# Two columns of a modulation as one-column products on TensorE in the opening of a transformer kernel

## The chip, the cores and the metric

The kernel runs on one core of a Trainium2 chip. The metric is the device time of one execution in microseconds. TensorE (PE) multiplies, VectorE (DVE), ScalarE (ACT) and GpSimd (POOL) do the rest, SyncE (SP) starts most transfers. Each engine works through its own queue in order and waits on semaphores for the others.

## What is computed

Two blocks over 256 tokens of 1024 channels. What matters here is the opening of the first, and the filter network of the second, which depends on no token and is computed at the very start:

```python
c_act = jax.nn.silu(c)
mod = c_act @ w_ada[l] + b_ada[l]                       # 1024 x 9216
(sh1, sc1, ga1, sh2, sc2, ga2, sh3, sc3, ga3) = jnp.split(mod, N_MOD, axis=-1)
h = modulate(rms_norm(x, g_pre_ff1[l]), sh1, sc1)       # h * (1 + scale) + shift
f = swiglu(h, w1_gate[l], w1_up[l], w1_down[l])
...
h = jnp.sin(sin_freq[0] * (z @ w1 + b1))                # filter network, 256 positions
h = jnp.sin(sin_freq[1] * (h @ w2 + b2))
h = jnp.sin(sin_freq[2] * (h @ w3 + b3))
h = (h @ w_out).reshape(L, HYENA_ORDER, 2, HYENA_WIDTH)
h = h * jnp.exp(-t[:, None, None, None] * jnp.abs(decay))
```

The filters' spectra follow, and their scale from the sums of squares. sh1 and sc1 are the "first two columns" of the modulation: without them the first feed-forward stage can't start. All weights are 32-bit numbers; each large product is made of three (high times high, high times low, low times high), for which ACT makes the high part of every weight panel (L184), and DVE the low part (L190).

## The kernel before

The order of all work is written out by hand, engine by engine; there is no planner. The opening has two tasks side by side.

The first is the modulation. `w_ada` comes as 72 panels of 128x1024 (512 KB), eight for each of its nine columns of 1024. SP loads the first 16 panels (columns sh1 and sc1) into a ring of five slots (L2345, in `load_ada`). DVE multiplies each by one value of `c_act` per partition and adds it to one of two accumulators, `acc0` (L739 for the first of a column, L731 for the others); the helper `spare()` puts one such addition wherever the order of the filter work leaves a place. At the end PE sums `acc0` over partitions: `sum_columns` (L769) takes each 128x128 piece as weights, and a column of ones as the moving operand. DVE adds the bias (L781, L783), makes two diagonal matrices with the tokens' norms (`diag_dve`, L375), and PE turns X with them (`norm_pe`, L431) into banks 4 to 7. ACT scales the result (`norm_act_rest`, L329), and DVE makes its low part (`low_dve`, L393 and L395), channel by channel. With those the first feed-forward stage starts (`first_up`, its products all at L206).

The second is the filter network, `spectrum_pe`, `spectrum_dve`, `spectrum_act` and `spectrum_pool`: three small layers (L1132, L1129) with their argument on DVE (L1162 to L1165, `round_off` at L881 to L884) and the sine on ACT (L1211); eight products for the taps (L1141, two times four, the network's 64 channels as rows); the taps times their decay (L1184), their sums and differences on POOL and DVE (L1252, L1199), squares on ACT (L1234) and their sums (L1258 to L1260, then `filter_sums_pe`, L1117); then two transforms, o = 0 and o = 1, of four quarters each (L1153), copied by ACT (L1243) and stored. Between the first and the second network layer stand the parameters of a state-space part (`params_dve`, 24 small DVE instructions), and behind the third `params_rest_dve` (L907 to L934, 21 of them).

In the first feed-forward stage (`ffn_pe`, `ffn_act`, `ffn_dve` with n = 0) DVE also adds up five further columns of the modulation (`ada_add_middle`, L731 again), for which POOL first clears accumulators and loads a row (`ada_middle_pool`, L837 and L827), and POOL makes tables from the parameters (`tables_pool`). One column sum in `ada_middle_pe`, at the end of the stage, is the same L769.

A product of 32-bit numbers that isn't made of three is two instructions in the trace (an LDWEIGHTS and a MATMUL each).

Of the kernel before, what the change touches and what calls it, by code (L numbers as in the profile page):

```python
# [81 lines left out]
def build_program(nc, panels, ada, cols, rows, sinks, ssm_mats, skip, tables, pool_mats, rope, near,  # L82
                  pool_w, decay, mlp_w, feats, x_in, out, spectrum, last_stage):
    ctx = ExitStack()
    with ctx:
# [40 lines left out]
        acc0 = region(4096, 2, D)  # L126
# [180 lines left out]
        def norm_act_squares(act, n, lo=0, hi=4):  # L307
            if n == 0:
                act.wait_ge(x_loaded, 16)
# [97 lines left out]

        def norm_pe(pe, n, first):
# [19 lines left out]
            for m in range(MT):  # L428
                pe.wait_ge(diag_done, 2 * n + m + 1)
                for k in range(KT):  # L430
                    mm = pe.matmul(turned_out(n, k)[:, m * P:(m + 1) * P], X[:, m, k * P:(k + 1) * P],  # L431
                                   diag[:, m, :], start=True, stop=True)
                    if m == MT - 1:
                        mm.then_inc(turned, 1)
# [30 lines left out]
        def ffn_pe(pe, n):  # L465
# [36 lines left out]

            norm_pe(pe, at, first_up)
            up(1)
            down(0, start=True)
# [73 lines left out]
        def ffn_dve(dve, n, order):  # L579
# [38 lines left out]
            dve_panels(dve, base + 3, 2)  # L618
            hidden(0)
# [114 lines left out]
        def ada_add(dve, a, dst):  # L734

            slot, k = a % ADA_RING, a % KT
            dve.wait_ge(ada_loaded[slot], 16 * (a // ADA_RING + 1))
            if k == 0:
                dve.tensor_scalar(dst, ada_ring[:, slot, :], c_act[:, 0:1], None,  # L739
                                  ALU.mult).then_inc(ada_used, 1)  # L740
            else:
                ada_multiply_add(dve, a, dst, ada_ring[:, slot, :], c_act[:, k:k + 1])

# [29 lines left out]
        def ada_first_pe(pe):  # L773
            for c in range(2):
                pe.wait_ge(ada_used, 8 * c + 8)
                sum_columns(pe, acc0[:, c, :], 7, 8 * c).then_inc(column_sums, 1)

        def ada_first_dve(dve, order):
            dve.wait_ge(column_sums, 2)
            for j in range(2):  # L780
                order(dve.tensor_tensor(mods[:, j, :], bank[7][:, 8 * j:8 * j + 8],  # L781
                                        col("b_ada", 8 * j, 8), ALU.add))
# [30 lines left out]
        def ada_middle_dve(dve, order):  # L813
            dve.wait_ge(column_sums, 6)
# [71 lines left out]
        def params_dve(dve, order):  # L886
# [3 lines left out]
            order(dve.tensor_scalar(pr(T2), pr(T0), 1.0 / 40320, None, ALU.mult))  # L890
            for n in (7, 6, 5, 4, 3, 2, 1):
                order(dve.scalar_tensor_tensor(out=pr(T2), in0=pr(T2), scalar=1.0 / math.factorial(n),
                                               in1=pr(T0), op0=ALU.add, op1=ALU.mult))
            order(dve.tensor_scalar(pr(T1), pr(T1), -126.0, 127.0, ALU.max, ALU.min))
            order(dve.tensor_scalar(pr(DT).bitcast(I32), pr(T1), 127.0, 8388608.0, ALU.add, ALU.mult))
# [211 lines left out]
        tap_sq = [region(at, 512) for at in (24576, 25088, 25600, 1024)]  # L1107
        decay_rows = region(0, 1024)
# [4 lines left out]
        def filter_sums_pe(pe, o):  # L1113

            pe.wait_ge(squares_added, o + 1)
            for c in range(4):
                mm = pe.matmul(bank[6][:, 4 * o + c:4 * o + c + 1], tap_sq[0][:, c * P:(c + 1) * P],  # L1117
                               ones[:, 0:1], start=True, stop=True)
# [3 lines left out]
        SPEC_BANKS = (1, 2, 3, 0)  # L1122

        def spectrum_pe(pe):
            pe.wait_ge(spec_loaded, 16 * 2)
            for layer in range(3):
                if layer:
                    pe.wait_ge(mlp_sin, layer)
                    pe.matmul(bank[7][0:64, 0:SEQ], mlp[0:64, 256 + 64 * layer:320 + 64 * layer],  # L1129
                              mlp_h, start=True, stop=True).then_inc(mlp_product, 1)  # L1130
                else:
                    pe.matmul(bank[7][0:64, 0:SEQ], mlp[0:33, 256:320], feat_t,  # L1132
                              start=True, stop=True).then_inc(mlp_product, 1)
            pe.wait_ge(mlp_sin, 3)
            pe.wait_ge(spec_loaded, 16 * 5)
            for o in range(2):
                for q in range(4):
                    m, d = q // 2, q % 2
                    if (o, q) == (1, 3):
                        pe.wait_ge(taps_done, 1)  # L1140
                    pe.matmul(bank[TAP_BANKS[o][q]][:, :], mlp_h[:, m * P:(m + 1) * P],  # L1141
                              filter_out[0:64, o * 1024 + d * 512:o * 1024 + d * 512 + 512],
                              start=True, stop=True).then_inc(taps_product, 1)
            for o in range(2):
                if o:
                    filter_sums_pe(pe, 0)
                pe.wait_ge(even_odd, 4 * o + 4)
                for q in range(4):

                    pe.wait_ge(*((spec_done, q + 1) if o else (taps_done, (2, 3, 4, 8)[q])))  # L1150
                    f, s = q // 2, q % 2
                    for m in range(MT):
                        mm = pe.matmul(bank[SPEC_BANKS[q]][:, :], dft[:, s, m, f * P:(f + 1) * P],  # L1153
                                       eo[:, 2 * m + s, :], start=m == 0, stop=m == MT - 1)
                    mm.then_inc(spec_product, 1)
            filter_sums_pe(pe, 1)

        def spectrum_dve(dve, order, spare):

            for layer in range(3):  # L1160
# [6 lines left out]
                if layer == 0:  # L1167
                    params_dve(dve, order)
                    dve.wait_ge(c_ready, 1)
                else:  # L1170
                    spare()
            params_rest_dve(dve, order)
            for _ in range(3):
                spare()
            for o in range(2):
                for q in range(4):
# [3 lines left out]
                    if o:  # L1180
# [4 lines left out]
                                            decays[:, m, d * 512:d * 512 + 512], ALU.mult)  # L1185
# [5 lines left out]
                    if q == 1:  # L1191
                        spare()
                for _ in range(3 * o):
                    spare()
                dve.wait_ge(taps_done, 4 * o + 4)
                if o:
                    dve.wait_ge(spec_product, 4)
# [3 lines left out]
                for _ in range(3):  # L1201
                    spare()
# [1449 lines left out]
```

## Time and profile before

| | |
|---|---|
| median of 3 runs | 1668.34 us (1663.57 to 1670.28) |
| profiled execution, its own time | 1668.2 us |
| its span in the profile | 1666.5 us |
| TensorE busy in the span | 1562.0 us (94%) |
| first product of the first feed-forward stage | at 79.50 us |

The profile is one execution. Its page gives busy times and the chain of work that ended last; the trace behind it can be asked for stretches, groups of instructions and single ones. Times are from the start of the span.

### The profile page before, as it was taken

What the parts mean: (1) busy time and instruction counts of PE and PEld (TensorE: products, weight loads), DVE (VectorE), ACT (ScalarE), POOL (GpSimd) and SP (SyncE); (2) the same over time, 40 slices, a digit from 0 to 9 for tenths busy, and PEclk for the clock granted to TensorE, in tenths of its full rate; (3) what the DMA queues carried; (4) which work ended last, traced back from release to release, by engine and by line L of the source; (5) the groups of instructions that cost most, each with busy time, mean ns of one, the idle gap of its engine ahead of it and who ended that gap; (6) DMA issues with size and microseconds to landing.
All of it is one profiled execution on the core that took longest, in us unless ns stands there. A gap on an engine that the chain in (4) does not pass through costs nothing.

```text
span 1666.5 us, 28244 instructions
## 1 busy us (share of the span) xinstructions
PE 1562.0 (94%) x10274; PEld 1423.6 (85%) x10274; DVE 1035.7 (62%) x1378; ACT 755.0 (45%) x1193; POOL 229.7 (14%) x278
## 2 busy tenths in 40 slices
PE   4899999887899999999999999999999989999997
PEld 1598999777689998999988689999999978889996
DVE  6789775783465565655556865555655557665554
ACT  3344553434454444544454354444444445454443
POOL 1479137370010000100000000000000000000000
PEclk9799999885899999999999999999999998999999
DMA  6688785421246654755543345554655533255551
GB/s 221 227 337 287 277 291 194 151 79 38 89 164 219 209 208 146 284 189 189 186 140 120 123 150 185 184 184 149 215 181 185 180 110 100 68 175 189 188 180 48
DMA packets 80279, 293.11 MB, mean 176 GB/s; under 512 B 9035, under 2 KB 9388, under 8 KB 79644
## 3 DMA queue, kind: packets, MB, share of 16 engines
q1 hardware_dynamic: 74432, 270.71, 48.4%
q0 software_dynamic: 4864, 19.35, 3.2%
q10 hardware_dynamic: 924, 2.25, 0.5%
q8 instruction: 39, 0.64, 0.2%
q14 instruction: 20, 0.16, 0.0%
HBM read 289.13 MB, written 3.15 MB: 175 GB/s over the span
## 4 chain that ended last, share of the span: by engine, by line
PE 85%; DVE 6%; ACT 4%; POOL 2%; issue 2%; DMA 1%; ACTq 0%; DVEq 0%; POOLq 0%
PE bank L206 75%; DVE w_lo L190 1%; PE bank L769 1%; PE bank L1793 1%; PE bank L431 1%; DVE arena L731 1%; POOL arena L1590 1%; ACT arena L301 1%; PE bank L2122 1%; PE bank L1806 1%; PE bank L1421 1%; PE bank L1153 1%; PE bank L404 1%; PE bank L2144 1%; DVE arena L671 0%
## 5 line engine op out<-in xcount | busy, mean ns | idle before, releaser
L206 PE MATMUL bank<-h_hi,w_hi 128*128 128x256 f32 x2376 | 685.3, 288 | 9.5 <-DVE h_lo L2252 3.0
L206 PE MATMUL bank<-h_lo,w_hi 128*128 128x256 f32 x2376 | 677.3, 285 | 0.0
L206 PE MATMUL bank<-h_hi,w_lo 128*128 128x256 f32 x2376 | 676.9, 285 | 0.0
L190 DVE TENSOR_TENSOR w_lo<-raw,w_hi 128x1024 fp32r<-128x1024 f32 x458 | 548.8, 1247 | 104.2 <-ACT w_hi L184 101.4
L206 PEld LDWEIGHTS bank<-h_hi,w_hi 128*128 128x128 f32 x2376 | 460.9, 194 | 22.6 <-DVE h_lo L395 5.0
L184 ACT ACTIVATE w_hi<-raw 128x1024 fp32r<-128x1024 f32 x458 | 456.8, 1049 | 36.6 <-PE bank L206 32.3
L206 PEld LDWEIGHTS bank<-h_lo,w_hi 128*128 128x128 f32 x2376 | 461.0, 194 | 5.5 <-issue 1.0
L206 PEld LDWEIGHTS bank<-h_hi,w_lo 128*128 128x128 f32 x2376 | 460.6, 194 | 0.0
L596 DVE TENSOR_TENSOR arena<-arena,bank 128x256 f32<-128x256 f32 x132 | 55.4, 420 | 265.1 <-PE bank L206 180.7
L206 PE MATMUL bank<-w_hi,f_hi 128*128 128x512 f32 x528 | 207.3, 393 | 0.0
L206 PE MATMUL bank<-w_hi,f_lo 128*128 128x512 f32 x528 | 207.0, 392 | 0.0
L206 PE MATMUL bank<-w_lo,f_hi 128*128 128x512 f32 x528 | 205.5, 389 | 0.0
L544 ACT ACTIVATE f_hi<-arena 128x256 fp32r<-128x256 f32 x132 | 55.2, 418 | 238.7 <-DVE arena L596 238.7
L336 POOL TENSOR_SCALAR stat<-stat 128x1 f32<-128x1 f32 x26 | 9.7, 374 | 1049.5 <-ACT arena L301 1048.7
L538 ACT ACTIVATE arena<-arena 128x256 f32<-128x256 f32 x88 | 36.8, 418 | 196.2 <-DVE arena L590 196.2
L206 PEld LDWEIGHTS bank<-w_lo,f_hi 128*128 128x128 f32 x528 | 99.2, 188 | 21.6
L206 PEld LDWEIGHTS bank<-w_hi,f_hi 128*128 128x128 f32 x528 | 99.7, 189 | 17.2
L206 PEld LDWEIGHTS bank<-w_hi,f_lo 128*128 128x128 f32 x528 | 99.7, 189 | 15.8
L731 DVE SCALAR_TENSOR_TENSOR arena<-arena,stat 128x1024 f32<-128x1024 f32 x70 | 100.2, 1431 | 1.2
L601 DVE TENSOR_TENSOR f_lo<-arena,f_hi 128x256 fp32r<-128x256 f32 x132 | 59.2, 448 | 52.2 <-ACT f_hi L544 52.2
L542 ACT ACTIVATE arena<-bank 128x256 f32<-128x256 f32 x44 | 16.9, 384 | 156.0 <-PE bank L206 156.0
L206 PE MATMUL bank<-w_hi,h_hi 128*128 128x512 f32 x116 | 48.6, 419 | 7.0 <-DVE h_lo L1714 2.8
(316 smaller groups left out, 1370.2 us busy)
## 6 DMA issues: line engine op xcount, KB each, us to landing
raw<-panels SPq DMA_DIRECT2D x458, 512.0 KB, 4.5
arena<-ada SPq DMA_DIRECT2D x56, 512.0 KB, 4.8
arena<-ada POOLq DMA_DIRECT2D x16, 512.0 KB, 3.9
spectrum<-arena POOLq DMA_DIRECT2D x2, 1024.0 KB, 7.7
arena<-rows POOLq DMA_DIRECT2D x4, 512.0 KB, 4.2
arena<-spectrum POOLq DMA_DIRECT2D x1, 2048.0 KB, 18.7
X<-x_in SPq DMA_DIRECT2D x1, 1024.0 KB, 5.1
arena<-decay ACTq DMA_DIRECT2D x2, 512.0 KB, 6.5
```

Source lines behind the costliest of these rows:

```text
L184: act.activation(w_hi[:, slot, :], raw[:, slot, :], ACT.Copy).then_inc(hi_ready, 1)
L190: dve.tensor_tensor(w_lo[:, slot, :], raw[:, slot, :], w_hi[:, slot, :].bitcast(F32), ALU.subtract).then_inc(lo_ready, 1)
L206: last = pe.matmul(out_ap, a, b, start=start and n == 0, stop=stop and n == 2)
L301: return act.activation(squares[:, q, :], source, ACT.Square, scale=D ** -0.5, accum_out=stat[:, at + q:at + q + 1])
L404: tr = pe.transpose(turned_out(n, k)[:, m * P:(m + 1) * P], X[:, m, k * P:(k + 1) * P], ident[:, :])
L431: mm = pe.matmul(turned_out(n, k)[:, m * P:(m + 1) * P], X[:, m, k * P:(k + 1) * P], diag[:, m, :], start=True, stop=True)
L538: act.activation(ffn_buf[:, f % 2, :], gate_buf[:, f % 2, :], ACT.Silu).then_inc(silu_done, 1)
L542: act.activation(ffn_buf[:, f % 2, :], gate_out(at, f), ACT.Silu).then_inc(silu_done, 1)
L544: act.activation(f_hi[:, f % 2, :], ffn_buf[:, 2 + f % 2, :], ACT.Copy).then_inc(f_hi_done, 1)
L596: dve.tensor_tensor(ffn_buf[:, 2 + f % 2, :], ffn_buf[:, f % 2, :], up_out(at, f), ALU.mult).then_inc(hidden_done, 1)
L601: dve.tensor_tensor(f_lo[:, f % 2, :], ffn_buf[:, 2 + f % 2, :], f_hi[:, f % 2, :].bitcast(F32), ALU.subtract).then_inc(f_lo_done, 1)
L731: dve.scalar_tensor_tensor(out=dst, in0=src, scalar=c, in1=dst, op0=ALU.mult, op1=ALU.add).then_inc(ada_used, 1)
```

## The change

The first two columns no longer go through DVE. For each of the 16 panels, as soon as it is loaded, PE takes its eight 128x128 pieces as weights and the column of `c_act` as the moving operand, and writes 128 single columns into bank 6; at the end one DVE reduction adds them up by eights. These products are spread over `spectrum_pe`: panels 0 and 1 behind the first layer, 2 to 4 behind the second, 5 to 7 behind the third, 8 and 9 behind the taps of o = 0, 10 to 12 ahead of the last tap product of o = 1, 13 to 15 behind the second to fourth quarter of the first transform.

The parameters on DVE are cut in three (`params_dve_0` ahead of the first layer, `_1` and `_2` behind the first and second), and their rest moves into the first feed-forward stage, behind its second group of splits. X is turned between the two transforms (`norm_turn_pe`), and ACT scales it and splits three panels ahead of the second squares and copies. The second transform uses banks 0, 1 and 2. The network's inputs, and the identity, go from ACT's queue to SP's, ahead of X; both rows of the decay are loaded early and have their own place. The sums of squares of the second filter come behind `first_up`.

```diff
-        def ada_first_pe(pe):
-            for c in range(2):
-                pe.wait_ge(ada_used, 8 * c + 8)
-                sum_columns(pe, acc0[:, c, :], 7, 8 * c).then_inc(column_sums, 1)
+        def ada_first_pe(pe, lo, hi):
+            for a in range(lo, hi):
+                slot, c, k = a % ADA_RING, a // KT, a % KT
+                pe.wait_ge(ada_loaded[slot], 16 * (a // ADA_RING + 1))
+                if a == 0:
+                    pe.wait_ge(c_ready, 1)
+                for j in range(KT):
+                    at = KT * (KT * c + j) + k
+                    mm = pe.matmul(bank[6][:, at:at + 1], ada_ring[:, slot, j * P:(j + 1) * P],
+                                   c_act[:, k:k + 1], start=True, stop=True)
+                mm.then_inc(ada_used, 1)
...
         def spectrum_pe(pe):
             pe.wait_ge(spec_loaded, 16 * 2)
@@
                     pe.matmul(bank[7][0:64, 0:SEQ], mlp[0:64, 256 + 64 * layer:320 + 64 * layer],
                               mlp_h, start=True, stop=True).then_inc(mlp_product, 1)
+                    ada_first_pe(pe, 3 * layer - 1, 3 * layer + 2)
                 else:
                     pe.matmul(bank[7][0:64, 0:SEQ], mlp[0:33, 256:320], feat_t,
                               start=True, stop=True).then_inc(mlp_product, 1)
+                    ada_first_pe(pe, 0, 2)
@@
                     if (o, q) == (1, 3):
+                        ada_first_pe(pe, 10, 13)
                         pe.wait_ge(taps_done, 1)
                     pe.matmul(bank[TAP_BANKS[o][q]][:, :], mlp_h[:, m * P:(m + 1) * P],
                               filter_out[0:64, o * 1024 + d * 512:o * 1024 + d * 512 + 512],
                               start=True, stop=True).then_inc(taps_product, 1)
+                if o == 0:
+                    ada_first_pe(pe, 8, 10)
             for o in range(2):
-                if o:
-                    filter_sums_pe(pe, 0)
                 pe.wait_ge(even_odd, 4 * o + 4)
                 for q in range(4):
 
-                    pe.wait_ge(*((spec_done, q + 1) if o else (taps_done, (2, 3, 4, 8)[q])))
+                    pe.wait_ge(*((spec_done, (4, 4, 4, 5)[q]) if o else (taps_done, (2, 3, 4, 8)[q])))
@@
                     mm.then_inc(spec_product, 1)
-            filter_sums_pe(pe, 1)
+                    if o == 0 and q:
+                        ada_first_pe(pe, 12 + q, 13 + q)
+                if o == 0:
+                    pe.wait_ge(taps_done, 8)
+                    pe.wait_ge(mods_done, 1)
+                    norm_turn_pe(pe, 0)
+                    filter_sums_pe(pe, 0)
...
+            if n == 0:
+                pe.wait_ge(spec_done, 8)
             norm_pe(pe, at, first_up)
+            if n == 0:
+                filter_sums_pe(pe, 1)
             up(1)
+            if n == 0:
+                pe.wait_ge(filter_sums, 1)
             down(0, start=True)
...
             dve_panels(dve, base + 3, 2)
+            if n == 0:
+                params_rest_dve(dve, order)
+                filter_sums_dve(dve)
             hidden(0)
...
+            act.wait_ge(decay_done, 4)
+            squares_of(0)
+            params_act(act)
+            params_rest_act(act)
+            copies(0)
+            act_panels(act, 0, 3)
+            norm_act_rest(act, 0)
+            act.wait_ge(tap_sums, 1)
+            squares_of(1)
+            act.wait_ge(spectrum_stored, 16)
+            copies(1)
...
             sp.dma_start(C[:, :], cols).then_inc(small_loaded, 16)
+            sp.dma_start(feat_t, feats).then_inc(spec_loaded, 16)
+            sp.dma_start(mlp_ws, mlp_w[:, 0:192]).then_inc(spec_loaded, 16)
+            sp.dma_start(ident[:, :], tables[0]).then_inc(x_loaded, 16)
             sp.dma_start(X[:, :, :], x_in.rearrange("(m p) d -> p m d", p=P)).then_inc(x_loaded, 16)
```

## Rows read from the trace of the kernel before

**Rows 1.** The page: busy time, share of the span and instructions of each engine.
```profile
PE 1562.0 (94%) x10274; PEld 1423.6 (85%) x10274; DVE 1035.7 (62%) x1378; ACT 755.0 (45%) x1193; POOL 229.7 (14%) x278
```

**Rows 2.** Stretches: busy us (instructions) of PE, PEld, DVE, ACT, POOL; granted clock; DMA.
```profile
0.00:79.50 79.50, 49.45 (x135) 27.27 (x135) 55.00 (x104) 27.25 (x47) 24.30 (x24) 0.89 0.69 235
79.50:100.00 20.50, 20.50 (x148) 19.00 (x149) 16.50 (x26) 12.11 (x17) 8.92 (x9) 1.00 0.57 199
100.00:160.00 60.00, 57.03 (x400) 53.24 (x399) 56.69 (x46) 28.01 (x39) 56.72 (x42) 1.00 0.93 334
```

**Rows 3.** The chain of waits to 150 us: start, us, what.
```profile
2.00 5.83 DMA arena<-mlp_w
...
66.33 5.53 PE bank L769 x32
...
79.50 61.27 PE bank L206 x432
```

**Rows 4.** Groups by line and form, 0 to 79.5 us: busy us, mean ns.
```profile
L731 DVE SCALAR_TENSOR_TENSOR arena<-arena,stat 128x1024 f32<-128x1024 f32 x14 | 22.0, 1569 | 0.7
...
L739 DVE TENSOR_SCALAR arena<-arena,stat 128x1024 f32<-128x1024 f32 x2 | 2.5, 1243 | 0.0
```

**Rows 5.** Timeline of PE, instructions merged: start, us, count.
```profile
23.18 14.02 PE L1141 MATMUL bank<-arena 64*128 64x512 f32 x16 [3.00 <-ACT arena L1211]
39.93 7.30 PE L1153 MATMUL bank<-arena 128*128 128x512 f32 x12 [2.74 <-POOL arena L1252]
...
66.20 5.65 PE L769 MATMUL bank<-ones,arena 128*128 128x1 f32 x32
...
267.07 8.74 PE L769 MATMUL bank<-ones,arena 128*128 128x1 f32 x64
```

**Rows 6.** Narrow stretches of PE's changes of pace, columns as in rows 2.
```profile
39.90:43.90 4.00, 3.97 (x5) 1.83 (x6) 3.90 (x3) 0.28 (x1) 3.92 (x2) 1.00 0.38 131
43.90:47.20 3.30, 3.30 (x8) 1.14 (x6) 3.14 (x5) 0.00 (x0) 2.00 (x2) 1.00 0.80 210
...
66.20:67.60 1.40, 1.40 (x15) 1.40 (x14) 0.17 (x1) 1.40 (x4) 0.00 (x0) 1.00 0.83 278
67.60:71.90 4.30, 4.25 (x21) 4.16 (x20) 0.02 (x1) 0.20 (x1) 2.61 (x3) 0.51 1.02 379
72.70:77.90 5.20, 5.20 (x24) 5.20 (x25) 0.15 (x1) 0.52 (x2) 0.00 (x0) 0.50 0.04 16
...
272.00:273.00 1.00, 1.00 (x9) 1.00 (x8) 0.00 (x0) 0.00 (x0) 1.00 (x2) 0.72 0.00 0
```

**Rows 7.** Transfers of the first 12 us: GB/s in 40 slices; X, us to landing.
```profile
GB/s 0 0 0 0 0 0 92 106 344 337 188 273 423 410 410 410 382 423 410 396 399 394 436 409 382 410 396 410 423 423 423 396 410 396 396 410 423 423 423 410
...
X<-x_in SPq DMA_DIRECT2D x1, 1024.0 KB, 5.1
```

**Rows 8.** Timeline of all engines, 0 to 66 us: one layer, table, parameters, copies.
```profile
2.59 1.28 ACT L2407 ACT_TABLE_LOAD   x1 [2.59 <-issue]
...
16.17 0.53 DVE L1162 TENSOR_SCALAR arena<-bank,C 64x256 f32<-64x256 f32 x1
...
18.60 0.42 ACT L1211 ACTIVATE arena<-arena 64x256 f32<-64x256 f32 x1 [1.92 <-DVE arena L1165]
...
28.07 0.17 DVE L934 TENSOR_TENSOR par<-par 128x16 f32<-128x16 f32 x1
...
53.91 2.04 ACT L1243 ACTIVATE arena<-bank 128x512 f32<-128x512 f32 x4
```

**Rows 9.** Timelines around the start of the first stage.
```profile
86.71 0.28 PE L206 MATMUL bank<-h_hi,w_hi 128*128 128x256 f32 x1
86.83 0.28 PE L206 MATMUL bank<-h_lo,w_hi 128*128 128x256 f32 x1
...
86.91 0.39 ACT L542 ACTIVATE arena<-bank 128x256 f32<-128x256 f32 x1 [2.57 <-PE bank L206]
...
96.89 3.50 DVE L190 TENSOR_TENSOR w_lo<-raw,w_hi 128x1024 fp32r<-128x1024 f32 x3 [2.27 <-DMA arena<-rows]
```

More of the change, by code:

```diff
@@ L406, in turn_pe, with norm_turn_pe @@
                 tr.then_inc(turned, 1)
+        def norm_turn_pe(pe, n):
+            for m in range(MT):
+                pe.wait_ge(diag_done, 2 * n + m + 1)
+                for k in range(KT):
+                    mm = pe.matmul(turned_out(n, k)[:, m * P:(m + 1) * P], X[:, m, k * P:(k + 1) * P],
+                                   diag[:, m, :], start=True, stop=True)
+                    if m == MT - 1:
+                        mm.then_inc(turned, 1)
         def norm_pe(pe, n, first):
@@ L427, in norm_pe @@
                 return
[L428 to L434, printed above, removed]
+            if n:
+                norm_turn_pe(pe, n)
             for k in range(KT):
@@ L771, in sum_columns @@
             return mm
[L773 to L782 removed]
+        def ada_first_pe(pe, lo, hi):
[9 more added lines that the diff above has]
+                mm.then_inc(ada_used, 1)
+        def ada_first_dve(dve, order):
+            dve.wait_ge(ada_used, ADA_FIRST)
+            order(dve.tensor_reduce(mods[:, 0:2, :].rearrange("p c j -> p (c j)"),
+                                    bank[6][:, 0:ADA_FIRST * KT].rearrange("p (n k) -> p n k", k=KT),
+                                    AX.X, ALU.add))
+            first = mods[:, 0:2, :].rearrange("p c j -> p (c j)")
+            order(dve.tensor_tensor(first, first, col("b_ada", 0, 16), ALU.add))
             dve.scalar_tensor_tensor(out=pre_scale[:, 0, :], in0=mods[:, 1, :], scalar=1.0,
@@ L1166, in spectrum_dve @@
                                   ALU.max).then_inc(mlp_arg, 1)
[L1167 to L1174, printed above, removed]
+                if layer < 2:
+                    params[layer + 1](dve, order)
+            diag_dve(dve, 0)
             for o in range(2):
@@ L1190, in spectrum_dve @@
                     ins.then_inc(taps_done, 1)
[L1191 to L1194, printed above, removed]
                 dve.wait_ge(taps_done, 4 * o + 4)
                 if o:
+                    ada_first_dve(dve, order)
                     dve.wait_ge(spec_product, 4)
@@ L1200, in spectrum_dve, with load_decay, magnitudes @@
                                       ALU.subtract).then_inc(even_odd, 1)
-                for _ in range(3):
-                    spare()
         def filter_sums_dve(dve):
             dve.wait_ge(tap_sums, 2)
-            dve.tensor_copy(filter_scale, bank[6][:, 0:8]).then_inc(filter_sums, 1)
+            dve.tensor_copy(filter_scale, bank[3][:, 0:8]).then_inc(filter_sums, 1)
+        def load_decay(act, o):
+            act.dma_start(decay_rows[:, o, :], decay[o:o + 1, :].partition_broadcast(P)).then_inc(
+                decay_loaded, 16)
         def spectrum_act(act, order):
+            def magnitudes(o):
+                act.wait_ge(decay_loaded, 16 * (o + 1))
+                if o == 0:
+                    load_decay(act, 1)
+                return act.activation(decay_rows[:, o, :], decay_rows[:, o, :], ACT.Abs)
             for layer in range(3):
@@ L1271, in spectrum_pool @@
             store(1)
+            ada_middle_pool(pool, order)
             pool.wait_ge(filter_sums, 1)
@@ L2402, in _ @@
             order = Order(act, act_order)
[L2403 to L2407 removed]
+            load_decay(act, 0)
             act.wait_ge(spec_loaded, 32)
@@ L2412, in _ @@
             act.dma_start(dft[:, 1, :, :], pool_mats[5]).then_inc(spec_loaded, 16)
-            act.dma_start(decay_rows, decay[0:1, :].partition_broadcast(P)).then_inc(decay_loaded, 16)
+            act.wait_ge(small_loaded, 16)
+            act.activation(c_act, col("c", 0, 8), ACT.Silu).then_inc(c_ready, 1)
             norm_act_squares(act, 0)
             spectrum_act(act, order)
-            norm_act_rest(act, 0)
             for at, (kind, n) in enumerate(stages):
@@ L2432, in _ @@
             order = Order(dve, dve_order)
-            ada_next = iter(range(ADA_FIRST))
-            def spare():
-                a = next(ada_next, None)
-                if a is not None:
-                    ada_add(dve, a, acc0[:, a // KT, :])
-            dve.wait_ge(small_loaded, 32)
-            spectrum_dve(dve, order, spare)
-            for _ in range(ADA_FIRST):
-                spare()
+            dve.wait_ge(small_loaded, 16)
+            spectrum_dve(dve, order)
             dve_panels(dve, 0, 3)
-            filter_sums_dve(dve)
-            ada_first_dve(dve, order)
-            diag_dve(dve, 0)
             low_dve(dve, 0, order)
```

76 lines of the change are left out of this document (27 added, 49 removed).

## The prediction

> **What bounds the kernel now.** I began with the page, which says that TensorE is busy for 94% of the span [rows 1], so time outside it can only be won where it waits. The table by stretches shows where that is: from 79.5 us to 160 us PE is all but always busy, and ahead of 79.5 us for 49.5 of 79.5 us [rows 2]. The chain of waits then names what sets the length of this opening: first the small weights of the filter network, whose transfer takes 5.8 us, then much of DVE's work, and at the end 5.5 us of column sums on PE (L769), after which the first 432 products of the first feed-forward stage follow in one piece [rows 3]. So the question is when the first product L206 can start (79.50 us now) and what is then still late. DVE spends 22.0 + 2.5 us on the sixteen additions [rows 4]. The reader should also see, in the timeline of PE, that a piece of work there has two prices: twelve 128x512 instructions took 7.3 us in one stretch, the first ones 0.85 us each, and sixteen 64-row ones took 14.0 us, 0.85 us each [rows 5]. The stretches show five instructions in 4.0 us before 43.9 us and, after it, eight in 3.3 us, overlaps counted [rows 6]. That is 1.2 and 2.4 GHz. The granted-clock column says 1.00 on both sides of 43.9 us, so for the first 44 us I go by the pace of the instructions and not by that column; from 66 us on the two agree.
>
> **The small products.** Each of the 16 panels of the first two columns now costs PE eight products of 128x128 weights and one moving column, two instructions each: 16 instructions. The kernel has the same shape in L769 and L1117. At 2.4 GHz they went 13 in the 1.40 us from 66.20, that is 0.108 us each; at 1.2 GHz 20 in the 4.3 us to 71.90, that is 0.213 us each [rows 6]. A panel is 1.73 us or 3.41 us, all sixteen 27.6 or 54.6 us. What goes is 24.5 us of DVE and 5.65 us of PE [rows 4, 5]. So the sign of the change hangs on the clock. What the engine did: it had the full clock after a dense stretch (L1153), and then it fell to 0.50 at about 67.6 us, some 2 us into the one-column products; in the run of 64 at 267.07 it fell after 5.4 us (a mean of 0.72 from 272 to 273 us), and these 64 took 8.74 us, not 6.9 [rows 5, 6]. In the opening it has not risen by 37.2 us, although the 64-row products filled 14 us of PE; it rises 4.0 us into the 128x512 products [rows 5, 6]. In the changed kernel nothing but one-column products, the small network layers and the 64-row products runs ahead of the first spectrum product. I therefore take 1.2 GHz up to there, and 2.4 GHz as the other bound.
>
> The Trainium skill ("TensorE: Matmul & The Clock Gate", the section on why this matters for your kernels) asks to keep TensorE continuously busy to get the full clock. Taken by busy time alone it would give the full clock early on, and so the other sum, the first rival below; the two falls in [rows 6] speak against reading it so.
>
> **The new order, step by step.** *Start.* The network's two inputs now go ahead of X. Their transfer takes 5.8 us with X's 1 MB ahead of it [rows 3], which is 2.5 us at the 0.4 MB a us of [rows 7]; with half of that (decay) beside it instead, the network should start near 6 us, not at 7.96 us. That gain is not kept: PE next wants the first panel. X lands at 6.4 us now; 0.5 MB of decay rows ahead of it and a panel behind it, at about 0.4 MB a us [rows 7], give 9.0 us (bounds 8 and 11). Silu, which the first panel's product waits for, stands behind ACT's wait for the two inputs, three issues of DMAs and its table (1.28 us [rows 8]); I estimate it done near 8 us, and it matters only past 9 us. The sines of the parameters move behind the exponentials on ACT, which then may load a table again (1.28 us); ACT waits for PE there, so nothing.
>
> *Up to the spectrum (1.2 GHz).* From 9.0 us PE has 13 panels (44.3 us), two layers at 1.1 us (2.2), and eight tap products at 2 x 0.85 us (13.7): it ends at 69.2 us, the 60.2 us behind the 9.0. Does it wait for another? A layer on DVE and ACT takes from 16.17 to 19.02 us, 2.9 us [rows 8], and PE has two or three panels (6.8 or 10.2 us) beside it: no. A panel's transfer of 1.3 us hides behind 3.41 us of product. The three parts of the parameters cost DVE what they cost before, but DVE is now idle there: nothing.
>
> *First spectrum.* It starts at 39.93 us in the kernel before [rows 5] and at 69.2 us in the changed one. Two quarters are 6.8 us at 1.2 GHz; with the clock rising after 4.0 us as now, 5.4 us. Two more at 1.7 us and panels 13 to 15 at 1.73 us: 8.6 us. PE is at 83.2 us. If the clock rises only after these it is 93.1 us, which I keep for the range.
>
> *Modulation and turning.* DVE's reduction, addition and product (about 0.2 us each, and 0.85 us lie between the last column sum and the first turning product now: 71.85 and 72.70 us) with the hand-over take 0.9 us: 84.1 us. The 32 turning instructions ran 5.2 us at 1.2 GHz before the clock rose [rows 6], at 0.21 us each, after a run of one-column products; the nearest row is this one, so 5.2 us for 24 and 0.8 us for the rest: 6.0 us (3.4 us if the clock holds). The sums of the first filter are eight more one-column instructions, 0.9 us: 91.0 us. The second spectrum, 16 instructions at 0.427 us, takes 6.8 us: 97.8 us, and its last copy on ACT (2.04 us for four [rows 8]) lets PE go at 98.4 us.
>
> *Who else could be late.* From their like in [rows 8]: ACT has three splits (3.3 us) from 82, the scaling (behind the turning, to 92), the squares (2.2 us) and then the copies: the first is done near 95, a bit ahead of where bank 0 is wanted. DVE subtracts 2.4 us, splits three panels (3.7 us with POOL quiet) and makes the low parts at 0.92 us each from about 90 us: done at 97.5 us. Both are just hidden; each late microsecond would show. It helps that the scaling (norm_act_rest) now comes ahead of the second squares and copies on ACT.
>
> *Start of the first stage.* The low parts are there, so the 48 first instructions go at 0.12 us instead of DVE's 0.92 us for six [rows 9]: 5.8 us, from 98.4 to 104.2 us; then the second filter sums, 0.9 us: 105.1 us. They end now at 86.8 us, just ahead of their first use on ACT at 86.91 [rows 9]. The end moves by +18.3 us.
>
> *Behind it.* The 21 instructions of the parameters' rest (4.5 us from 23.73 to 28.24 us) [rows 8] move to DVE between the splits and the first hidden tile; queued behind them are that tile and the splits of three panels, and PE waits for the tile in the down product. DVE reaches them some 4 us earlier against PE than before, and loses the 2.27 us that it now waits for the accumulators' rows [rows 9]. So nothing; at worst 4.5 us, since DVE is busy for 56.7 of the 60 us from 100 us on [rows 2]. POOL's tables wait for these parameters, the pow and the memsets, and start at about the same distance from the stage's start. Zero, between -2 and +4.5 us.
>
> **Sum.** The profiled execution took 1668.2 us (span 1666.5 us), as the median of 1668.34 us. 1668.2 + 18.3 = 1686.5; I predict 1686 us.
>
> **The rivals.** *Full clock early* (0.09): being busy without a gap suffices and the panels cost 1.73 us each from about 9 us. It saves 13 x 1.68 us, 1.1 us of layers, 6.8 us of taps, 2.0 us in the first spectrum and 2.6 us in turning, less about 1 us for landings: 33.4 us, 1653 us, faster. For it: PE has no gap. Against: both falls during such products [rows 6]. It decides if the clock rises before panel 5: from there on 18 us are saved.
> *Clock up with the first taps* (0.10): these run behind a full PE now, not behind a gap. Saved from 42.4 us on: taps 4.8, panels 8 to 12 8.4, first spectrum 2.0, together 15.3 us: 1671 us, no change to be told. Against: 14 us of these very products didn't raise it [rows 5].
> *Never up in the first spectrum, or DVE the bound behind it* (0.05 beyond my range): 83.2 becomes 93.1 us, and with 4.5 us of parameters and 2 us of a later start it is 1703 us.
> *PE at 1.2 GHz* as summed has 0.76: from 1681 us (turning at full clock, -2.6 us, first panel at 8 us, -1, and the -2 us behind the start) to 1702 us.
>
> **How the numbers follow.** Likeliest 1686 us. The range from 1670 to 1702 us reaches down to the case of the taps (half of its 0.10 lies in it) and leaves out the early full clock and the slow end, 0.19 in all. About 0.5% (8 us) can be told from no change by this measurement. Faster 0.10 (the early full clock, and 0.01 of the taps' case if it falls well), same 0.11 (the rest of the taps' case and 0.02 of mine, if two of its small gains meet others that I don't see), slower 0.79 (0.74 of mine and the 0.05 of the slow end).
>
> **What would show it.** Right: PE instructions of panels 0 to 12 some 0.21 us apart, the layers two and three at about 16 and 27 us, first spectrum product near 69 us, first L206-like product near 98 us, DVE idle through much of the first 65 us. Wrong: a pace of 0.11 us in the panels, which takes the whole sum down; a first stage that starts well before 90 us; or a new gap of PE behind the second spectrum or between 105 and 160 us.

## The result and the profile after

The changed kernel takes 1694.7 us (median of four runs, 1690.15 to 1698.42) against 1668.28 us (four runs, 1663.57 to 1670.28): a ratio of 1.0166, 95% interval 1.0138 to 1.0194. It is slower, by 26 us in the medians and by 22.0 us in the two profiled executions (1690.15 against 1668.2 us). Two single runs of other kernels below, one of 5251.48 us (experiment 6) and one of 4826.04 us (the kernel before, beside experiments 4 and 6 to 8), are slow ones and are left out of the ratios.

The page of the changed kernel, busy time of each engine:

```profile
PE 1596.5 (95%) x10498; PEld 1460.5 (86%) x10498; DVE 1014.1 (60%) x1362; ACT 757.9 (45%) x1195; POOL 226.9 (13%) x278
```

Against [rows 1], PE has 34.5 us more and DVE 21.6 us less. The timeline of PE (start, us, line, count, and in brackets the wait before it):

```profile
6.17 1.08 PE L1154 MATMUL bank<-arena 33*64 33x256 f32 x2 [6.17 <-DMA arena<-mlp_w]
14.47 6.99 PE L784 MATMUL bank<-stat,arena 128*128 128x1 f32 x32 [7.22 <-DMA arena<-ada]
21.39 1.11 PE L1150 MATMUL bank<-arena 64*64 64x256 f32 x2
22.43 10.40 PE L784 MATMUL bank<-stat,arena 128*128 128x1 f32 x48
...
44.12 7.19 PE L1165 MATMUL bank<-arena 64*128 64x512 f32 x8
...
73.90 2.07 PE L1165 MATMUL bank<-arena 64*128 64x512 f32 x2
75.89 5.75 PE L1177 MATMUL bank<-arena 128*128 128x512 f32 x8
81.48 1.84 PE L784 MATMUL bank<-stat,arena 128*128 128x1 f32 x16
...
91.63 3.81 PE L412 MATMUL bank<-diag,X 128*128 128x128 f32 x32 [1.30 <-issue]
...
96.09 7.11 PE L1177 MATMUL bank<-arena 128*128 128x512 f32 x16
103.89 0.39 PE L205 MATMUL bank<-h_hi,w_hi 128*128 128x256 f32 x1 [0.69 <-ACT arena L1263]
...
294.23 9.75 PE L772 MATMUL bank<-ones,arena 128*128 128x1 f32 x64
```

From 14.47 us on there is no wait of PE until the modulation is summed at 90.3 us. A panel ahead of the first spectrum takes 3.5 us (48 instructions in 10.4 us); behind its second quarter, at 81.48 us, it takes 1.84 us. The four tap products of o = 0 (eight instructions) take 7.19 us, about half of the 14.02 us that all eight took before [rows 5]: the taps ran at 1.2 GHz already in the kernel before. Narrow stretches of the first spectrum's instructions alone (busy us and instructions of PE, PEld; granted clock; DMA share, GB/s):

```profile
75.89:80.10 4.21, 4.21 (x5) 1.85 (x6) 1.00 0.55 224
80.10:81.48 1.38, 1.38 (x4) 0.38 (x2) 1.00 0.00 0
```

And the turning (busy us and instructions of PE, PEld, DVE, ACT, POOL; granted clock; DMA):

```profile
91.60:95.40 3.80, 3.77 (x34) 3.80 (x35) 3.80 (x5) 1.78 (x4) 0.41 (x1) 1.00 0.76 291
```

Five 128x512 instructions in 4.2 us, then the other three of the first eight in 1.4 us (an instruction that lies across the edge is counted on both sides): the clock goes from 1.2 to 2.4 GHz at about 80.1 us, 4.2 us into the spectrum, while its column says 1.00 on both sides, as in [rows 6]. In the turning it stays up.

Three marks split the difference: the end of the first stage's first 48 products (in the changed kernel with the second filter's sums behind them), the start of the 64 column sums at the end of the stage (267.07 us in [rows 5]), and the end of the span.

| profiled execution | first mark | to the 64 sums | to the end of the span |
|---|---|---|---|
| before | 86.8 | 180.3 | 1399.4 |
| after | 110.7 | 183.5 | 1394.3 |
| difference | +23.9 | +3.3 | -5.1 |

The last column scatters: in the twelve profiled executions of this study it is 1394.3 to 1394.5 us in three, and 1398.6 to 1401.5 in the other nine, of kernels that share this code. Runs of the changed kernel lie in two groups too (1690.2 and 1691.9, 1697.5 and 1698.4 us). So 22.0 us understates the change by some 5 us, and the median's 26 us agrees with 23.9 + 3.3.

### The profile page after: what moved, and what is told of

Read it like the earlier page. It is cut to its first block, busy times and chain, and to the rows that moved or that the text cites. A ratio compares the mean times of both kernels' runs of the same rounds, so it can differ in the third digit from the quotient of the medians.

```text
span 1688.5 us, 28668 instructions
## 1 busy us (share of the span) xinstructions
PE 1596.5 (95%) x10498; PEld 1460.5 (86%) x10498; DVE 1014.1 (60%) x1362; ACT 757.9 (45%) x1195; POOL 226.9 (13%) x278
## 4 chain that ended last, share of the span: by engine, by line
PE 86%; DVE 6%; ACT 4%; issue 2%; POOL 2%; DMA 1%; SPq 0%; DVEq 0%; ACTq 0%; POOLq 0%
PE bank L205 71%; PE bank L784 3%; DVE w_lo L189 2%; PE bank L1177 1%; PE bank L1165 1%; PE bank L1826 1%; PE bank L412 1%; POOL arena L1623 1%; ACT arena L300 1%; DMA arena<-ada 1%; PE bank L1839 1%; PE bank L1063 1%; PE bank L1454 1%; PE bank L772 1%; DVE arena L744 1%
## 5 line engine op out<-in xcount | busy, mean ns | idle before, releaser
L183 ACT ACTIVATE w_hi<-raw 128x1024 fp32r<-128x1024 f32 x458 | 456.6, 1049 | 34.5 <-PE bank L205 31.5
L205 PEld LDWEIGHTS bank<-w_lo,f_hi 128*128 128x128 f32 x528 | 99.2, 188 | 21.6
L744 DVE SCALAR_TENSOR_TENSOR arena<-arena,stat 128x1024 f32<-128x1024 f32 x56 | 78.1, 1394 | 0.5
L784 PEld LDWEIGHTS bank<-stat,arena 128*128 128x128 f32 x256 | 50.6, 306 | 14.0 <-DMA arena<-ada 8.1
```

What stands on the lines that cost most here:

```text
L183: act.activation(w_hi[:, slot, :], raw[:, slot, :], ACT.Copy).then_inc(hi_ready, 1)
L205: last = pe.matmul(out_ap, a, b, start=start and n == 0, stop=stop and n == 2)
L744: dve.scalar_tensor_tensor(out=dst, in0=src, scalar=c, in1=dst, op0=ALU.mult, op1=ALU.add).then_inc(ada_used, 1)
L784: mm = pe.matmul(bank[6][:, at:at + 1], ada_ring[:, slot, j * P:(j + 1) * P], c_act[:, k:k + 1], start=True, stop=True)
```

## The experiments

**1. All but the small products.** The sixteen additions and the column sums are back (`ada_first_pe` is the old one again, ahead of the turning), all else of the change stays.

```diff
-                    ada_first_pe(pe, 0, 2)
...
+                    ada_first_pe(pe)
                     pe.wait_ge(mods_done, 1)
...
+                if layer: spare()
+            spare(3)
...
+                    spare(16)
```

> All of the change but its small products: the sixteen panels go back to DVE (L731's like), the column sums to PE ahead of the turning. Theory of the small products at 1.2 GHz: the opening is bound by DVE again, with 4.5 us of parameters moved out of it and the turning ahead of the second transform; the first product of the first stage starts at 62 to 68 us (79.5 before, 103.9 changed), and the time is 1652 to 1660 us. Rival (the rest of the change, its new order and waits, carries a good part of the loss): slower than before, 1675 us or more.

Measured: 1662.56 us, ratio 0.9964 (0.9941 to 0.9987). Faster, so the rival is out, but by less than expected: the theory gave 1652 to 1660 us, and a first product of the first stage at 62 to 68 us, where it starts at 72.56 us. Its PE timeline, and the chain of waits (start, us, what):

```profile
13.84 1.11 PE L1152 MATMUL bank<-arena 64*64 64x256 f32 x2 [6.53 <-ACT arena L1259]
17.99 1.11 PE L1152 MATMUL bank<-arena 64*64 64x256 f32 x2 [3.04 <-ACT arena L1259]
23.18 14.02 PE L1164 MATMUL bank<-arena 64*128 64x512 f32 x16 [4.09 <-ACT arena L1259]
37.13 9.48 PE L1174 MATMUL bank<-arena 128*128 128x512 f32 x16
46.45 1.84 PE L783 MATMUL bank<-ones,arena 128*128 128x1 f32 x16
54.40 3.57 PE L783 MATMUL bank<-ones,arena 128*128 128x1 f32 x16 [6.10 <-DVE arena L745]
58.70 5.41 PE L413 MATMUL bank<-diag,X 128*128 128x128 f32 x32 [0.73 <-DVE pre_scale L797]
```

```profile
3.01 7.89 DMA X<-x_in
...
11.46 2.02 ACT arena L301 x7
13.48 0.31 ACT arena L1259
13.82 7.72 DMA arena<-decay
21.62 1.07 ACT arena L1255
22.71 0.42 ACT arena L1259
```

The network's inputs do arrive early (6.23 us, not 7.96), but ACT squares X ahead of the first sine, and X now comes later; then it waits for the second decay row ahead of the third sine. The taps start at 23.18 us, exactly as before [rows 5]. What is won is won later: the first mark is at 79.36, not 86.8 us.

**2. The small products alone, in the kernel before**, at all the places of the change.

```diff
+                    ada_first_pe(pe, 3 * layer - 1, 3 * layer + 2)
...
-            for _ in range(ADA_FIRST):
-                spare()
```

> The kernel before with the small products alone, at the same places of PE's order; parameters, turning and transfers stay. Theory of the small products: PE paces the opening at 3.4 us a panel from about 9.6 us on; 60 us up to the first spectrum product (near 70 us), 14 us to the second, and the turning and scaling behind it: first stage near 102 us, 1688 to 1696 us in all. Rival (the loss comes from the rest): near 1668 us or faster.

Measured: 1693.79 us, ratio 1.0152 (1.0121 to 1.0183), as expected (the first stage starts at 105.99 us, some 4 us later than expected). One part alone gives nearly the whole loss, and the rest of the change doesn't bring its 6 us back. Here the panels start at 8.93 us without a wait, and the first spectrum at 70.35 us.

**3. Is it the clock? Idle dense products between the small ones.** Nine products of 128x128 by 128x256 whose result nobody reads go into the wait for the first panel, and one ahead of each four small products of panels 0 to 12.

```diff
+        def fill(pe):
+            pe.matmul(bank[6][:, 256:512], ones[:, :], C[:, 0:256], start=True, stop=True)
...
                 for j in range(KT):
+                    if a < 13 and j % 4 == 0:
+                        fill(pe)
```

> The changed kernel with more work on PE: nine idle products of 128x256 ahead of the first panel, where PE waits anyway, and one ahead of every fourth small product of panels 0 to 12 (26 in all, 0.43 us each at 2.4 GHz), into unused columns of bank 6. Theory of the clock: it rises before the first panel and holds; small products 0.11 us an instruction in place of 0.21, taps 0.43 in place of 0.85; first spectrum product near 56 us in place of 75.9, 1668 to 1676 us. Rival (the small products cost the same whatever the clock, or one-column products pull it down all the same): 11 to 22 us more than the changed kernel, 1705 us or more.

Measured: 1711.33 us, ratio 1.0264 (1.0233 to 1.0295): the rival's number. Its PE timeline, and a stretch of it (columns as for the turning above):

```profile
16.02 0.95 PE L789 MATMUL bank<-stat,arena 128*128 128x1 f32 x8
16.83 0.73 PE L777 MATMUL bank<-C,ones 128*128 128x256 f32 x2
17.36 1.70 PE L789 MATMUL bank<-stat,arena 128*128 128x1 f32 x8
```

```profile
17.40:30.00 12.60, 12.60 (x50) 11.11 (x48) 3.70 (x15) 1.47 (x2) 0.00 (x0) 0.50 0.51 195
```

The idle products did raise the clock (eight small instructions in 0.95 us), and it fell again at 17.4 us, with PE busy without a gap, and stayed at 0.50 up to 60 us. The trial didn't hold the clock, so it doesn't say what the small products would cost at 2.4 GHz.

**4. Twice as many.** One idle product ahead of each two small ones (`j % 2`), 61 in all.

> As the run with the dense fill, but with an idle 128x256 product ahead of every second small product of panels 0 to 12 (52 in all): as much dense as small work, the share at which the clock held in the first transform of the changed kernel. If the clock then holds: eight small instructions in 0.95 us, a panel 3.4 us with its fill, taps 0.43 us, first spectrum product near 67 us (75.9 changed), 1680 to 1688 us, though PE does 22 us more work at that clock. If it falls all the same: a panel 6.8 us, first spectrum product near 119 us, 1730 to 1740 us.

Measured: 1682.38 us (two runs), ratio 1.0077 (1.0058 to 1.0096), as expected. Its PE timeline:

```profile
14.58 0.50 PE L789 MATMUL bank<-stat,arena 128*128 128x1 f32 x4
14.95 0.68 PE L777 MATMUL bank<-C,ones 128*128 128x256 f32 x2
15.46 0.50 PE L789 MATMUL bank<-stat,arena 128*128 128x1 f32 x4
...
43.57 3.70 PE L1172 MATMUL bank<-arena 64*128 64x512 f32 x8
...
68.76 3.70 PE L1184 MATMUL bank<-arena 128*128 128x512 f32 x8
```

Everything up to the first spectrum goes at twice the pace, the taps too (3.70 us, not 7.19). Four small instructions and an idle product take 0.88 us, the four alone 0.43 at this pace: the 52 behind the first panel's arrival are 23.4 us of added work. From there to the first spectrum it is 54.2 us; less 23.4, the kernel's own work takes 30.8 us, against 61.4 in the changed kernel. With more work in the same place the kernel is 9.1 us shorter (span 1679.4 against 1688.5). So the clock makes half of what the small products cost. By an estimate the span would be 1679.4 less 23.4, about 1656 us, if that pace could be had without the idle products and no other engine were late; no run shows that.

**5. The rest of the parameters back into DVE's idle time**, ahead of the last taps.

```diff
+                    if (o, q) == (1, 3):
+                        params_rest_dve(dve, order)
...
-                params_rest_dve(dve, order)
                 filter_sums_dve(dve)
```

> The changed kernel with the 21 instructions of the parameters' rest on DVE ahead of the last tap product of o = 1, where DVE idles from 64 to 76 us. Theory that they cost PE a wait in the first stage: the 183.6 us from the end of the second filter sums to the column sums of that stage become 180, 3 to 4 us less in all. Rival (they are hidden, and the 3.3 us are the clock's): within 1 us of it in the opening, and the stage as long as before within its scatter.

Measured: 1691.2 us, ratio 1.015 (1.0114 to 1.0185). From the first to the second mark it takes 182.0 us, 1.5 less than after and 1.8 more than before. Beside the other profiled executions this says little of the parameters and much of the clock:

| first to second mark | parameters in the stage | us | granted clock |
|---|---|---|---|
| before | no | 180.3 | 0.98 |
| experiment 5 | no | 182.0 | 0.97 |
| experiments 1, 3 and 7 | yes | 182.2 to 182.3 | 0.97 |
| experiment 2 | no | 184.2 | 0.96 |
| after, experiments 4, 6, 8, 9, 10 | yes | 183.5 to 183.8 | 0.96 |

At 0.97 the parameters in the stage make 0.3 us at most, at 0.96 the version without them is the longest. So the parameters aren't shown to cost anything there, and the rival was right about the stage.

**6. First sine ahead of the squares of X**, in the version of experiment 1.

```diff
-            norm_act_squares(act, 0)
             spectrum_act(act, order)
...
                 if layer == 0:
+                    norm_act_squares(act, 0)
                     magnitudes(0)
```

> The run with the rest of the change alone, and ACT's squares of X behind the first sine instead of ahead of it (the squares wait for X until 10.9 us, and the second network layer with them until 13.84 us). Theory that the network's chain and DVE's additions behind it bound that opening: second layer near 10.5 us, first additions 3 us earlier, first stage 2 to 4 us earlier: 1657 to 1661 us. Rival (the panels' landing near 14.5 us bounds DVE): within 1 us, 1662 us.

Measured: 1662.11 us (1661.72 without the run of 5251.48 us), ratio 0.9943 (0.9922 to 0.9963). That is the rival's time and not the theory's. The second layer starts at 9.84, not 13.84 us, and the taps at 22.19, not 23.18 us. Its chain shows why:

```profile
9.38 0.42 ACT arena L1259
9.86 10.70 DMA arena<-decay
20.64 1.06 ACT arena L1255
```

The second decay row, wanted only behind the taps, is waited for by ACT ahead of the third sine, and takes up three of the four microseconds. So the time came out as the rival said, by another transfer than the one it named.

**7. Three of the sixteen panels on PE, behind the first spectrum** (in the version of experiment 6), where the clock has risen. The edit's main part:

```diff
+            for a in range(ADA_ON_DVE, ADA_FIRST):
+                for j in range(KT):
+                    mm = pe.matmul(bank[6][:, at:at + 1], ada_ring[:, slot, j * P:(j + 1) * P],
+                                   c_act[:, k:k + 1], start=True, stop=True)
```

> The last one, with panels 13 to 15 as small products on PE behind the first transform, where PE waits for DVE and has 2.4 GHz; 0 to 12 stay on DVE. Theory that small products pay where PE idles at the full clock: 1.7 us a panel on PE, three additions of 1.3 to 2.1 us off DVE's chain, modulation ready 4 to 6 us earlier than in the run before it: 1652 to 1657 us, the fastest here. Rival (they come at 1.2 GHz, or wait for their transfers): no faster than the run before it, 1659 us or more.

Measured: 1665.01 us, ratio 0.9972 (0.9959 to 0.9984), a miss; the rival was right. Its PE timeline:

```profile
46.52 1.84 PE L785 MATMUL bank<-ones,arena 128*128 128x1 f32 x16
48.23 9.69 PE L797 MATMUL bank<-stat,arena 128*128 128x1 f32 x48
57.78 3.55 PE L802 MATMUL bank<-ones,arena 128*128 128x1 f32 x16
```

The first 16 one-column instructions still go at 2.4 GHz; 48 more of them take 9.69 us, not 5.2, and the sums behind them are at 1.2 GHz too. Even three panels don't hold the clock. But nor does the wait that they fill: in experiment 6, where PE stands still in most of this place, the granted clock is 0.58 from 47.5 to 52.5 us and 0.50 behind it. So the expectation's premise, a wait at full clock, was wrong, and the loss is the small products' own 9.7 us ahead of the second column's sums.

**8 and 9. Why is the first panel late?** Experiment 8 loads the first decay row behind ACT's other transfers; experiment 9 also puts the network's inputs and the identity back on ACT's queue, X second on SP's.

```diff
-            load_decay(act, 0)
             act.wait_ge(spec_loaded, 32)
...
+            load_decay(act, 0)
             act.wait_ge(small_loaded, 16)
```

> The changed kernel with the first decay row loaded behind ACT's other transfers, as before, so that 0.5 MB less stands ahead of X and the first panel. Theory that the first panel's landing (14.47 us in the changed kernel's profile, 9.63 in a second one with the same opening) sets the start of PE's chain: small products start at or before 9.7 us, and the time is 2 to 5 us under the changed kernel's, 1690 to 1693 us. Rival (landing is a matter of chance between queues): the start stays anywhere from 9 to 15 us and the median at 1694 us.

> The changed kernel, with its first transfers in the queues of the kernel before: the identity and the network's two inputs on ACT's queue, X second on SP's, and the decay's row on ACT's behind the transform's matrices. Theory A (the five transfers ahead of the first panel, with SP issuing three more, made it late): the first of the small products starts by 10 us instead of 14.47 us, and as TensorE has no slack up to the first spectrum, the time falls by 3 to 5 us, to 1689 to 1692 us. Rival B (where the first panel lands scatters from run to run whatever the order; two other versions of the changed kernel showed 9.6 and 13.1 us): the start lies anywhere between 9 and 15 us, and the median stays within 2 us of 1694.7 us.

Measured: 1695.66 us, ratio 1.0159 (1.0143 to 1.0175), and 1693.22 us, ratio 1.0146 (1.0120 to 1.0173). Both times are the rival's: neither order brings the 2 to 5 us. The small products start at 13.11 and at 11.53 us; in the latter the wait ends with ACT's silu and not with the panel. Experiment 5, whose opening is the changed kernel's, started them at 9.63 us and then waited for a panel until 14.25 us.

The landing of the panel itself says more than that start. The first panel's issue, its size and the us to its landing, in the changed kernel (issued at 3.48 us) and in experiment 9 (issued at 1.79 us):

```profile
arena<-ada SPq DMA_DIRECT2D x1, 512.0 KB, 11.0
```

```profile
arena<-ada SPq DMA_DIRECT2D x1, 512.0 KB, 6.2
```

With the old order of the transfers it is 6.2 us in all three profiled executions (before, experiments 2 and 9). With the new one it is 6.1 to 11.9 us in eight (after and experiments 1, 3 to 7 and 10), and with the decay row moved alone 9.6 us (experiment 8). So the order does make the panel late and its landing scatter, against the second rival; which of the moved transfers does it isn't shown. Experiment 9 gets its panel at 8.0 us and loses the rest of the gain by waiting for silu. Its timeline:

```profile
11.53 6.96 PE L784 MATMUL bank<-stat,arena 128*128 128x1 f32 x32 [2.56 <-ACT stat L2444]
...
72.92 6.33 PE L1177 MATMUL bank<-arena 128*128 128x512 f32 x8
...
89.24 6.71 PE L412 MATMUL bank<-diag,X 128*128 128x128 f32 x32 [1.30 <-issue]
...
104.39 0.39 PE L205 MATMUL bank<-h_hi,w_hi 128*128 128x256 f32 x1 [0.69 <-ACT arena L1263]
```

Its turning (columns as for the turning of the changed kernel):

```profile
89.24:95.50 6.26, 6.26 (x30) 6.26 (x31) 5.05 (x6) 2.10 (x5) 0.39 (x1) 0.51 0.83 290
```

Of the 3 us that it is ahead at the first spectrum 0.6 are lost in it and the rest in the turning, which the clock's fall now hits (6.71 us, not 3.81).

**10. Experiment 1 with 27 idle products in PE's waits**, to have its taps and spectrum at full clock: 8 and 5 ahead of the second and third layer, 6 ahead of the taps, 8 behind them.

> The version without the small products (the sixteen additions back on DVE, all else of the change kept), with 27 idle products of 128x128 by 128x256 in TensorE's waits of the opening: 8 ahead of the second network layer, 5 ahead of the third, 6 ahead of the taps, 8 behind them. Theory A (TensorE's clock also sets part of this version's opening): the taps go at some 0.46 us an instruction, not 0.88, which takes 6.7 us off them, the first spectrum goes at 0.43 from its start and ends 3 to 7 us earlier than 46.6 us; the end moves by 2 to 7 us, 1656 to 1661 us. Rival B (DVE's additions and the sines set it; the products of the second column's sums already wait 6.1 us for DVE): the taps get faster, but the second column's sums still start within 1.5 us of 54.4 us and the time is 1661 to 1664 us. Rival C: the idle products come late into the network's chain, the taps start behind 24 us, and the time is over 1664 us.

Measured: 1663.52 us, ratio 0.9962 (0.9948 to 0.9976), as Rival B said. Its PE timeline and two stretches (columns as for the turning of the changed kernel):

```profile
22.54 11.37 PE L1170 MATMUL bank<-arena 64*128 64x512 f32 x16 [2.65 <-ACT arena L1266]
...
53.06 3.57 PE L783 MATMUL bank<-ones,arena 128*128 128x1 f32 x16 [4.47 <-DVE arena L745]
```

```profile
22.50:26.00 3.50, 3.46 (x7) 1.52 (x8) 3.29 (x3) 3.48 (x4) 0.00 (x0) 0.89 0.76 225
26.00:39.80 13.80, 13.80 (x26) 7.53 (x25) 13.50 (x14) 7.55 (x11) 9.10 (x5) 0.53 0.61 202
```

The taps start at full clock and lose it within 3.5 us, behind a wait of 2.65 us. The second column's sums, which wait for DVE's additions, start 1.3 us earlier, and the turning gives that back (6.42 us, not 5.41).

## Why the prediction was right

1694.7 us lies in the range, 9 us above the 1686 that it gave, and the cause is the one it named: products at 1.2 GHz that fill PE up to the first spectrum. Of the 9 us the first panel makes most and the clock in the first stage the rest. By its steps:

*Price of a small product.* 3.41 us a panel was forecast. The 60.2 us of work from the first panel to the first spectrum took 61.4 us (75.89 less 14.47). Experiment 2 shows that this part alone makes the loss, experiment 4 that the clock makes half of the price. At full clock this stretch is 30.8 us, so the rival of the early full clock had a fair price and a wrong condition: the engine was busy without a gap, and the clock didn't rise. Experiments 3 and 7 show it falling in such work after it had been up. By the Trainium skill ("TensorE: Matmul & The Clock Gate", the section on why this matters for your kernels) keeping the engine continuously busy is what is asked for; the 61.4 us from 14.47 us on disagree, if it is read by busy time alone.

*First panel.* The step that was mis-sized: 14.47 us against 9.0, and against the bound of 11. It had been worked out from bytes at 0.4 MB a us. In the chain the panel's transfer takes 10.95 us from its issue at 3.48 us. All transfers together moved 385 GB/s from 2.8 to 10 us, near what was assumed, and then 240 GB/s up to 14.4 us, with the DMA engines as busy as before (a share of 1.01 and 1.02). The order of the transfers is part of the cause (6.2 us from issue to landing with the old one, 6.1 to 11.9 with the new); decay's half megabyte alone isn't shown to be (9.6 us without it in experiment 8, inside that scatter). The rest is open.

*Taps, first spectrum, modulation.* 14.0 us from the spectrum to the last panel were forecast, 14.4 measured; 0.9 us for the modulation against 1.3. The clock rose 4.2 us into the spectrum (4.0 forecast).

*Turning.* 6.0 us against 3.8: the clock held, which the prediction had kept as its other case (3.4 us). It was 3.8 to 6.7 us in the versions run here, by where the clock's fall met it, so that this term came out low is in part luck. First filter's sums and second spectrum with its hand-over 8.5 (forecast 8.3), and from the stage's start to the end of the second filter sums 6.8 (6.7).

*Together.* +5.5 for the panel, +1.2 behind it, +0.4 and +0.4, -2.2 for the turning, +0.2: the second sums end at 110.7 us, not 105.1. The move of the end of the opening is +23.9 us where +18.3 was forecast.

*Behind the start.* Zero between -2 and +4.5 us was forecast, for DVE's added work; +3.3 was measured, and not for that. The stretch between the first two marks as one window each, before and after, and PE's waits of over 0.5 us in both (engine and line, what it waited for, us in total, times, longest):

```profile
86.80:267.07 180.27, 176.80 (x1239) 165.92 (x1238) 147.08 (x139) 91.63 (x129) 107.72 (x115) 0.98 0.85 296
```

```profile
110.68:294.23 183.55, 180.02 (x1239) 169.15 (x1239) 147.86 (x151) 91.25 (x128) 108.26 (x115) 0.96 0.82 286
```

```profile
PE bank L206 <- DVE w_lo L190: 3.0, 1, 3.0
```

```profile
PE bank L205 <- DVE w_lo L189: 3.0, 1, 3.0
```

The same 1239 instructions and the same wait, but a granted clock of 0.96 for 0.98: 2% of 181 us is 3.6 us, the whole difference. It lies behind that wait: in the three stretches of 20 us from 164 us on it is 0.96, 0.76 and 0.94, where the kernel before has 1.00, 0.84 and 0.99 from 140 us on. What is missing to 1.00 adds up to 6.8 us after and 3.4 us before: 3.4 us more, for the 3.3 us measured. The table of experiment 5 shows the same in all twelve profiled executions: the stage's length goes with its granted clock. The clock stays down longer; why was not tried. DVE has the parameters behind it at 113.3 us.

*The additions' side.* The prediction counted 24.5 us of DVE as removed and gave them no worth, since the opening would then hang on PE. Experiment 1 shows what they cost where they stay: with the additions back, PE waits for them (6.10 us at 54.40 us), and it is still 32 us faster than the changed kernel.

The best versions are those of experiments 1, 6 and 10, 0.4% to 0.6% below the kernel before; their medians are within 2 us and their intervals overlap, so which of them is best stays open.

## What to carry to other kernels

Before work is moved to TensorE, price it at the clock that the engine will have there, and take that from the pace of like instructions in the trace, not from the engine's busy share. A single moving column doesn't make a product cheap: at 2.4 GHz a one-column instruction took 0.108 us, and one with 128 columns, in the turning, 0.114 us (32 from 91.63 to 95.27 us), with the weight load busy all the time in both. So sixteen instructions per panel took 3.4 us at 1.2 GHz, against 1.57 us on average for the same panel on VectorE, and even at full clock (1.73 us) nothing is won on the engine's own time. And small products don't hold the clock for what stands behind them: it fell in them in experiments 3 and 7, and they left it at 1.2 GHz up to the first spectrum. The taps and the start of the first spectrum lost nothing by that, for they ran at 1.2 GHz in the kernel before too [rows 5, 6].

## What the runs showed of the hardware

- TensorE stayed at 1.2 GHz through 61.4 us without a gap, of one-column, 64-row and small-network products. One idle 128x256 product to four small ones didn't hold 2.4 GHz (experiment 3), one to two did (experiment 4).
- The granted-clock column says 1.00 in the opening while the pace is that of 1.2 GHz (before, after, experiment 1). Where the clock first falls, the column is right from then on: 0.50 from 17.4 us in experiment 3.
- 64-row products neither raised the clock (14.0 us in [rows 5]) nor held it in experiment 10 (0.53 from 26 us on); between idle products, in experiment 4, they ran at 2.4 GHz.
- A transfer of 512 KB issued at 3.48 us landed 10.95 us later, while all the transfers together moved 385 GB/s and from 10 us on 240 GB/s at the same busy share. The same panel in the old order took 6.2 us in three executions out of three: bytes ahead of it alone don't give its landing.
